# Expert results added into the residual rows in DRAM by the scatter, and router logits formed from unnormalised rows

## What is computed

```python
x = x + gt_a * out                                   # out = concat(gla, pooled) @ w_out
h2 = rmsnorm(x, norm2_g) * (1.0 + sc_m) + sh_m
x = x + gt_m * hier_moe(h2, w_router_group, w_router_expert, w_expert_in, w_expert_out)
return rmsnorm(x, final_norm_g)

def hier_moe(h, w_rg, w_re, w_e_in, w_e_out):        # 4 groups of 8 experts, D_EXPERT = 256
    pg = softmax(t @ w_rg); gp, gi = top_k(pg, 1)    # one group per token
    le = (t @ w_re)[group gi]
    ew, ei = top_k(softmax(le), 2); weights = gp * ew / sum(ew)
    # y[token] = sum over its two experts of weight * (silu(a) * u) @ w_out[e],  a, u = split(t @ w_in[e])
```

## Time and profile before

| | |
|---|---|
| median of three runs | 1640.46 us (1639.87 to 1645.15) |
| the profiled execution, its own time | 1644.79 us |
| its span | 1642.9 us |
| mean granted TensorE clock | 0.963 |
| busy: TensorE / VectorE / ScalarE / GpSimd | 89% / 43% / 23% / 19% |
| moved by DMA | 232.59 MB |

### The profile page before, as it was taken

The page is one execution under the profiler, slowest core; times in us unless marked ns, Lnnn a source line. Parts: engine busy times, 40 slices in busy tenths (PEclk is TensorE's granted clock), DMA queues, the critical chain, the costliest instruction groups (busy, mean ns, idle before and its releaser), DMA issues. The chain is left out here.

```text
span 1642.9 us, 22231 instructions
## 1 busy us (share of the span) xinstructions
PE 1461.7 (89%) x8638; PEld 985.6 (60%) x8638; DVE 703.2 (43%) x1226; ACT 378.8 (23%) x799; POOL 316.9 (19%) x269
## 2 busy tenths in 40 slices
PE   5999999999999979989999999999989977888782
PEld 4864446884544457778888778673757764332220
DVE  5252344123369957775332144310354445332324
ACT  3224445104333333322100122301231010000001
POOL 3420021520007255534630000000000001111110
PEclk9999999999999979999999999999998978999996
DMA  5237110303112124414332040422033257999995
GB/s 186 81 121 237 52 54 24 103 26 128 52 52 77 59 71 130 131 52 168 127 129 77 0 129 26 73 72 67 22 123 111 95 204 310 425 421 426 422 378 219
DMA packets 119545, 232.59 MB, mean 142 GB/s; under 512 B 13329, under 2 KB 103023, under 8 KB 110483
## 3 DMA queue, kind: packets, MB, share of 16 engines
q1 hardware_dynamic: 114115, 220.54, 37.5%
q0 software_dynamic: 5184, 8.55, 1.4%
q10 hardware_dynamic: 144, 2.10, 0.3%
HBM read 223.65 MB, written 17.84 MB: 147 GB/s over the span
## 5 line engine op out<-in xcount | busy, mean ns | idle before, releaser
L962 PE MATMUL psv<-arena 128*128 128x256 f32 x1008 | 221.5, 379 | 2.1 <-issue 2.1
L962 PEld LDWEIGHTS psv<-arena 128*128 128x128 f32 x1008 | 191.1, 190 | 30.2 <-issue 4.4
L924 PE MATMUL psv<-arena,wslot 128*128 128x512 f32 x384 | 170.8, 598 | 1.8 <-DVEq L2214 1.8
L1634 ACT ACTIVATE arena<-pss 128x512 f32<-128x512 f32 (+1 forms) x157 | 84.8, 540 | 330.2 <-PE pss L924 276.3
L1549 PE MATMUL pss<-arena 128*64 128x512 f32 x432 | 118.0, 618 | 14.5 <-DMA arena<-w_expert_in 11.9
L924 PEld LDWEIGHTS psv<-arena,wslot 128*128 128x128 f32 x384 | 71.1, 190 | 85.5 <-issue 83.0
L924 PE MATMUL pss<-arena 128*128 128x256 f32 (+1 forms) x384 | 113.6, 453 | 5.8 <-ACTq L152 3.1
L2230 DVE TENSOR_TENSOR arena<-arena,psv 128x512 f32<-128x512 f32 x66 | 45.4, 687 | 163.5 <-PE psv L962 161.3
L2445 DVE SCALAR_TENSOR_TENSOR arena<-psv,ccols,arena 128x510 f32<-128x510 f32 (+1 forms) x96 | 71.9, 749 | 59.9 <-ACT arena L1801 56.8
L924 PEld LDWEIGHTS pss<-arena 128*128 128x128 f32 x384 | 71.7, 190 | 41.1 <-issue 28.4
L924 PE MATMUL psv<-wslot,arena 128*128 128x256 f32 x416 | 93.1, 385 | 3.0 <-DMA wslot<-w_in 2.6
(11 more groups left out here) (346 smaller groups left out, 2014.5 us busy)
## 6 DMA issues: line engine op xcount, KB each, us to landing
arena<-w_expert_in SPq DMA_DIRECT2D x27, 2048.0 KB, 26.8
wslot<-w_in SPq DMA_DIRECT2D x32, 1024.0 KB, 5.5
arena<-w_expert_out SPq DMA_DIRECT2D x32, 1024.0 KB, 27.3
wslot<-w_ada SPq DMA_DIRECT2D x18, 1024.0 KB, 5.4
arena<-w_in SPq DMA_DIRECT2D x10, 1024.0 KB, 6.8
wslot<-w_expert_in SPq DMA_DIRECT2D x5, 2048.0 KB, 21.5
arena<-w_ada SPq DMA_DIRECT2D x6, 1024.0 KB, 9.0
arena<-x SPq DMA_DIRECT2D x8, 512.0 KB, 7.9
```

What stands on the lines that cost most here:

```text
L924: m = mm(o, l, r, start=(n == 0), stop=(n == len(pairs) - 1))
L962: m = mm(o[:, j * HALF_T:(j + 1) * HALF_T], l[:, c, j * P:(j + 1) * P], r[:, c, :], start=new and j == 0 and c == 0, stop=j == 1 and c == ...
L1634: L.did(A(dst, src, func, **kw), s[sig] if sig else None, [s["free_s"]])
```

## The change

**Scatter with addition.** `y_dram` is gone. `x3_dram` has one more (spare) row, and the scatter of a pair's results adds into it. The router's weight of a slot, `w_slot`, is made by a second table product and multiplied in where `hid` is formed, so the rows need no weight later. A pair is now the experts `i` and `i + 16`, which lie in different groups, so no token is twice in one scatter. One index table serves gather and scatter. At the end four blocks of `x3_dram` are loaded once the scatters have landed, and VectorE no longer adds.

**Logits from unnormalised rows.** `turn_x3` turns `x3` itself; `h3T` has the gain only. The logits are scaled by the token's inverse root when they are evicted, and the shift's part, `shift @ wrt`, is a row `lshift` made once before. The turning of tile `t - 1` now stands amid the column blocks of tile `t`.

```diff
-        y_dram = scratch("y_dram", 2 * SEQ + 1, DM)
-        x3_dram = scratch("x3_dram", SEQ, DM)
+        x3_dram = scratch("x3_dram", SEQ + 1, DM)
@@ sync
-        win_src = a["w_expert_in_2"][0].rearrange("(i x) (p c) n -> i x p c n", x=2, p=P)
+        win_src = a["w_expert_in_2"][0].rearrange("(x i) (p c) n -> i x p c n", x=2, p=P)
-            sp.wait_ge(s["xn_saved"], 16 * (NT + 1))
-            sp.wait_ge(s["x3_saved"], 16 * NT)
+            sp.wait_ge(s["rows_saved"], 2 * 16 * (NT + 1))
...
-            sp.wait_ge(s["index_ready"], 2)
+            sp.wait_ge(s["index_ready"], 3)
...
-            sp.wait_ge(s["win_used"], rounds * NP)
-            for t in range(NT):
-                load(x3[:, t, :], x3_dram[t * P:(t + 1) * P, :], "x3_saved")
             for k in range(2):
-                sp.wait_ge(s[f"st_y{k}"], rounds * (NP // 2 * 16) + 16)
-            for t in range(NT):
-                for k in range(2):
-                    sp.dma_start(ygat[:, k, t, :], y_dram[k * SEQ + t * P:k * SEQ + (t + 1) * P, :])\
-                        .then_inc(s["ygat_ready", t], 16)
+                sp.wait_ge(s[f"st_y{k}"], rounds * (HALF * 16) + 16)
+            for t in range(NT):
+                sp.dma_start(x3[:, t, :], x3_dram[t * P:(t + 1) * P, :]).then_inc(s["x3_back", t], 16)
@@ tensor
+            pe.wait_ge(s["ld_wrt"], 32)
+            o = bank("v")
+            product(o[:, 0:NG + NE], [(mod[:, 24 + c, 0:1].broadcast_to([P, P]), wrt[:, c, :]) for c in range(KC)])\
+                .then_inc(s["full_v"], 1)
...
             def turn_x3(t):
-                L.need(s["x3_ready"])
-                turn_features(x3n[:, t, :])
+                L.need(s["x3_raw"])
+                turn_features(x3[:, t, :])
...
             for t in range(1, NT):
-                for b in range(4):
+                for b in range(2):
                     token_tile("v", wo2[b], t, catT)
                 turn_x3(t - 1)
-                if t >= 2:
-                    logits(t - 2)
-            pe.drain().then_inc(s["phase"], 1)
-            logits(NT - 2)
+                for b in range(2, 4):
+                    token_tile("v", wo2[b], t, catT)
+                if t == NT - 1:
+                    pe.drain().then_inc(s["phase"], 1)
+                logits(t - 1)
             turn_x3(NT - 1)
             logits(NT - 1)
...
+            for table in (tok_at, wgt_at):
...
@@ gpsimd
             def scatter(k, rows_):
                 nc.gpsimd.indirect_dma_start(
-                    y_dram, bass.IndirectOffsetOnAxis(ycol[:, k:k + 1], 0), rows_, None,
-                    bounds_check=2 * SEQ, oob_is_err=False).then_inc(s[f"st_y{k}"], 16)
+                    x3_dram, bass.IndirectOffsetOnAxis(ycol[:, k:k + 1], 0), rows_, None,
+                    bounds_check=SEQ, oob_is_err=False, compute_op=ALU.add).then_inc(s[f"st_y{k}"], 16)
@@ vector
             def logits(t):
                 b = full()
-                L.did(V.tensor_copy(lg[:, t, :], b[:, 0:NG + NE]), s["free_v"])
+                L.did(V.scalar_tensor_tensor(lg[:, t, :], b[:, 0:NG + NE], ss[:, t:t + 1], lshift, ALU.mult, ALU.add),
+                      s["free_v"])
...
             def list_tokens(c0, c1):
                 b = full()
-                L.did(V.tensor_scalar(row_f[:, c0:c1], b[:, c0:c1], float(NOWHERE), spare, ALU.add, ALU.min), s["free_v"])
-                L.did(V.tensor_scalar(row_k[:, c0:c1], row_f[:, c0:c1], float(SEQ), float(-SEQ), ALU.is_ge, ALU.mult))
-                add(row_k[:, c0:c1], row_k[:, c0:c1], row_f[:, c0:c1])
-                if c0:
-                    L.did(V.tensor_copy(y_index[:, c0:c1], row_f[:, c0:c1]))
-                L.did(V.tensor_copy(index[:, c0:c1], row_k[:, c0:c1]), s["index_ready"])
-                if not c0:
-                    L.did(V.tensor_copy(y_index[:, c0:c1], row_f[:, c0:c1]))
+                L.did(V.tensor_scalar(index[:, c0:c1], b[:, c0:c1], float(NOWHERE), spare, ALU.add, ALU.min),
+                      s["index_ready"], [s["free_v"]])
...
             dve.wait_ge(s["ld_gs"], 48)
+            mul(wpick, pick, ewt.unsqueeze(3).broadcast_to([P, NT, 2, NE]))
+            for t in range(NT):
+                mul(wgt_at[:, t], wpick[:, t].unsqueeze(2).broadcast_to([P, 2, ROUNDS, NE]),
+                    rround[:, 2 * t:2 * t + 2, :].unsqueeze(3).broadcast_to([P, 2, ROUNDS, NE]), s["table_ready"])
+            b = full()
+            L.did(V.tensor_copy(w_slot, b[:, 0:ROUNDS * NP]), s["free_v"], [s["index_ready"]])
...
-                L.did(V.tensor_tensor(hid[:, k, :], pss[:, (s0 + job) % 4, DE:2 * DE], sil[:, k, :], ALU.mult),
-                      s["hid_ready"], [s["free_s"], s["sil_used"]])
+                L.did(V.scalar_tensor_tensor(hid[:, k, :], pss[:, (s0 + job) % 4, DE:2 * DE], w, sil[:, k, :],
+                                             ALU.mult, ALU.mult), s["hid_ready"], [s["free_s"], s["sil_used"]])
```

More of the change, by code:

```diff
@@ L410, in build @@
         assert top[0] <= 24 * K
+        lshift = at(ARENA - NG - NE, NG + NE)
         xe = at(24 * K, 2, KC, P)
@@ L829, in _ @@
             save(NT - 1)
-            load(xn_dram[SEQ:, :].rearrange("o (p n) -> (o p) n", p=KC), zero[0:KC, :], "xn_saved")
+            for rows_ in (xn_dram, x3_dram):
+                load(rows_[SEQ:, :].rearrange("o (p n) -> (o p) n", p=KC), zero[0:KC, :], "rows_saved")
             for x in range(2):
@@ L1529, in _ @@
                 m.then_inc(s["full_v"], 1)
-            o = bank("v")
-            for t in range(NT):
-                L.need(s["table_ready"])
-                for k in range(2):
-                    slots = tok_at[:, t, k, :, :].rearrange("p r (i x) -> p (r i) x", x=2)
-                    for x in range(2):
-                        m = mm(o[x * CAP:(x + 1) * CAP, 0:ROUNDS * NP], rplaced[:, 2 * t + k, :], slots[:, :, x],
-                               start=(t == 0 and k == 0), stop=(t == NT - 1 and k == 1))
-            m.then_inc(s["full_v"], 1)
+            for table in (tok_at, wgt_at):
+                o = bank("v")
+                for t in range(NT):
+                    L.need(s["table_ready"])
+                    for k in range(2):
+                        for x in range(2):
+                            m = mm(o[x * CAP:(x + 1) * CAP, 0:ROUNDS * NP], rplaced[:, 2 * t + k, :],
+                                   table[:, t, k, :, x * NP:(x + 1) * NP], start=(t == 0 and k == 0),
+                                   stop=(t == NT - 1 and k == 1))
+                m.then_inc(s["full_v"], 1)
             def turn_xg(o, k, h):
```

94 lines of the change are left out of this document (45 added, 49 removed).

## The result

| | before | changed |
|---|---|---|
| median | 1640.46 us (1639.87 to 1645.15, 5 runs) | 1649.41 us (1646.67 to 1650.88, 5 runs) |
| profiled execution, its span | 1644.79, 1642.9 | 1650.18, 1648.3 |
| mean granted clock | 0.963 | 0.963 |

The ratio is 1.0056 (95% interval 1.0038 to 1.0073): slower, by more than the 0.3% that can be told from no change. The forecast was 1636.8 us.

What follows compares the result with a forecast made beforehand. The prediction took DMA, saturated with expert weights, to bound the loop. Its terms, -4.6 (router), -8.1 (end) and +9.0 (adding scatters), summed to -3.7: 1641.1 us against the profile's 1644.8, 1636.8 against the median; range 1625 to 1660.

Steps and rivals of the forecast that it cites:

- three places: Where time counts: the way to the first gather, the loaded expert loop, and the end.
- The nearly empty stretch: DMA before the next load at 1386.0 us: 10 slices of 1.5 us from about 1376 us nearly empty.
- paced by weights, not by products: Expert loop: DMA at full share with 423 GB/s, so bytes added there cost time.
- The last logits, the first gather: Router: last logits at 1344.6 or 1346.3 us against 1350.8, gather issued at 1359.5 instead of 1365.3.
- 4.6 us earlier: First gather lands at 1369.9 us, 4.6 us earlier (3 to 6), and the next load follows at 1381.4.
- rival 3: Router's gain does not arrive: first gather flies 11.7 us or VectorE's new tables end after it; 1641 us, chance 0.10.
- `lshift` at 1.87 us: Router: extra TensorE product of eight steps of 36 columns, priced like one logits, 1.87 us.
- Part 3: Loaded loop: each adding scatter costs one further transfer, 0.67 us for 13.5 scatters, 9.0 us lost.
- Part 2: The end: four of eight loads and two VectorE additions per tile removed, 9.1 us earlier before the scatter's cost.
- Net 8.1: The end: 9.1 us saved, less 1 us for the last scatter's addition.
- estimated at 1 us more, a third of the whole: The end: the last scatter, 2.9 us before, must also read what it adds to, 1 us more.
- Rival 1: Loop: the chain of scatters becomes the bound, from a landing time of 14.4 us; 1655 us, chance 0.27.

Runs made afterwards that it cites:

- e6: The changed kernel with the third pair's weights queued only when both first gathers have landed; 1642.24 us, 1.0004 of the kernel before.
- e9: The kernel before with logits from unnormalised rows and the third pair's weights held until both first gathers landed; 1638.69 us, 0.9986.
- e3: The kernel before with everything in the change except the logits from unnormalised rows; 1646.64 us, 1.0039.
- e8: Kernel before with logits from unnormalised rows, pair 0's product ahead of pair 1's turning, third pair's weights held until the first gather landed; 1637.66 us, 0.9984.
- e10: The changed kernel with a writing scatter and, beside each scatter, an extra gather of the same rows; 1647.49 us, 1.0036 of the kernel before.
- e1: The changed kernel with a scatter that writes instead of adds; 1633.14 us, 0.996 of the kernel before.
- e11: e9 with the final additions shared: ScalarE scales one row, GpSimd adds it, VectorE adds the other; 1641.7 us, 1.0013 of the kernel before.

## Why the prediction was wrong

The sum was -3.7 us; the profiles give +5.4, the medians +9.0. Step by step:

1. **What bounds the kernel.** Right in that three places counted, and nearly all of the difference lies in them. The nearly empty stretch of the earlier trace rows is seven slices, not ten, about the 10 us that the text then used. And "paced by weights, not by products" holds only for the later loop: a full queue cost nothing while the ring was ahead, up to some 74 us after `s0`.
2. **The last logits, the first gather.** Forecast 1344.8 to 1346.5 and 1359.5, measured 1343.76 and 1358.21: slightly better than forecast. The landing at 1369.9 is the forecast to a tenth, by luck: an issue 1.3 us earlier than forecast and a flight of 11.7 us instead of 10.4 cancelled.
3. **"4.6 us earlier" for the load behind pair 0.** This step failed: 0.3 us. The sum followed pair 0's rows and never asked when pair 1's rows land, though TensorE's order has their turning ahead of pair 0's product, and though the text says itself that the weights of pairs 1 and 2 queue on SyncE. The text worked out when those weights are through, 1377.7 (measured 1377.3), and drew from it only that the next load is not hindered. The second gather lands about then, so its earlier issue gave little: TensorE waited 3.2 us for it, the product started 2.8 us later than the first rows allowed, and it took 1.6 longer at the lower granted clock. It is rival 3's outcome by another mechanism: neither a flight of 11.7 us for the first gather nor VectorE's tables held it up, the second gather did. e6 and e9 show it for the wait by taking the third pair's load out of the way: the second gather then flies 4.1 and 4.4 us. For the 1.6 us they do not, since the product stays slow in e6 (8.78 us). VectorE's tables were covered, as forecast; in e3, without the router part, they end just where the turning starts.
4. **`lshift` at 1.87 us, and nothing for the clock.** The work was priced, and rightly as work on the path. That the price falls ahead of everything else, in a stretch where TensorE is just coming up to its higher level (before, 0.77 granted from 1236 to 1246 us, 0.89 to 1256, 1.00 behind), was not seen. The stretch was 1.8 us longer in the pair of profiles and 8.5 in e8's, where the granted clock was 0.50; how much of the 8.5 is the product's doing no run separates. It can explain some of why the medians differ by more than the profiles.
5. **Part 3, +9.0 us.** The mechanism was right, the size a little low. 0.67 us for each scatter became 4% more of 16 engines' time, 8 us in 200 (13.1% less 9.1%), and e10, which does literally what the forecast took as its price, has the same share within a point and TensorE's last product at the same time, though not the same scatters. s0 to s13, the 13 steps that were counted, grew by exactly 9.0 (193.9 to 202.9), which is partly luck, for s13 to s14 grew by another 2.8, which the sum did not have, and the growth did not come step by step. Over all profiles s0 to s14 is 219.0 us in the six kernels with the addition and 208.7 in the eleven without an addition or e10's gather, 10.3 us apart.
6. **Part 2, "Net 8.1".** The saving was right: from the landing of the last scatter 12.2 us instead of the forecast 13 to 14, 10.2 less than before, and e1 gives 10 as well; ScalarE paced it, 1.5 us for each tile after the first. The other term was mis-sized: "estimated at 1 us more, a third of the whole" measured 3.0 for the last scatter (5.96 against 2.92), and 1.0 again since the last scatter waits for the one before it. Net 6.2. For a transfer that stands alone the addition nearly doubles the time; the same doubling stood in part 3 and should have been used here.
7. **Rival 1, the chain of scatters.** It did not decide, though it came near. GpSimd waited for a scatter in 7 of 13 turns, 13.1 us in all. In those turns the one before landed 11.5 to 14.1 us after its issue (from 1429.48 to 1443.60 us, for one), under the 14.4 from which the chain would bind, and the DMA share stayed full. Neither TensorE nor VectorE waited for a scatter in the loop, and TensorE waited more for weights, 21.4 us instead of 15.4 in 1400 to 1625 us. This is the case of the forecast, not of the rival: bytes, not turns.
8. **The numbers.** The range 1625 to 1660 held the 1649.4. The chances did not: slower was given 0.28, almost all of it for rival 1, while the terms that in fact made it slower were taken as small. 4.3 us (the router's load), 2.8 (the loop to s14) and 1.9 (the last scatters) all lay on one side and make, within rounding, the 9.1 by which the pair of profiles differs from the forecast. The medians differ by 3.6 more than the profiles, of which `lshift`'s variable price can be a part; the rest is not settled.

The Trainium skill (Collectives: The Full Stack, "The bandwidth ceiling: the fold count and why AG ≠ RS ≠ AR") counts the adding step of a collective as two reads and one write at half the rate. The trace agrees with the half rate: 5.96 us against 3.14 for the same rows alone, and e10's separate read and write cost the loop about what the addition does (TensorE's last product 222.8 and 222.6 us after `s0`, against 212.1).

## What to carry to other kernels

Follow every buffer that the first consumer waits for, in the order of the engine's text, and not only the first: a transfer that is issued earlier into a full queue may land no earlier, as here about when the queue was through, and an engine whose order has it ahead of the critical step passes its lateness on. In a loop that DMA paces, an addition in the transfer is paid like a second transfer of the same rows; it pays only if the work that it saves at the end is longer than that sum (here some 10 us against some 16). A small product belongs in a wait of TensorE; ahead of a long busy stretch it cost some 2.5 us in the mean here, for 1.9 of work.

## What the runs showed of the hardware that was not expected

- An adding scatter also costs GpSimd more: 1.60 us to issue instead of 1.02 (16 of each, changed kernel and e1).
- The same kind of gather (128 slots) flew 4.2 to 14.0 us in the changed kernel; the second one landed 2.3 us before the queued weights were through, and with the third pair's weights held back it flew 3.9 to 4.4 us.
- TensorE's clock varied between executions in the same stretch by more than an edit of 2 us does: `M` to `G` took 19.4 to 28.3 us in the ten profiles that run the same instructions there.
- Of a GpSimd addition and a VectorE step on 128x1024 tiles the one that started second was late by about the overlap: 1.99 us became 3.06 for GpSimd, 1.28 became 2.70 for VectorE (e11).
